# The last six units of a query projection in two load buffers, and expert rows 4 and 5 in the other two

## The reference

```python
def peer_ffn(h, w_q, keys_1, keys_2, u_table, v_table):
    q = jnp.dot(h, w_q).reshape(b, s, PEER_HEADS, 2, PEER_HALF)      # 2048 x 2048
    s1 = jnp.einsum('bshd,kd->bshk', q[:, :, :, 0], keys_1)          # 128 keys a side
    s2 = jnp.einsum('bshd,kd->bshk', q[:, :, :, 1], keys_2)
    v1, i1 = lax.top_k(s1, PEER_TOPK); v2, i2 = lax.top_k(s2, PEER_TOPK)
    ...                                                              # best 16 of the 256 pairs
    expert = jnp.take_along_axis(cand_index, top_pos, axis=-1)       # 8 heads x 16 a token
    gate = jax.nn.softmax(top_score.astype(jnp.float32), axis=-1)
    ...
        u = jnp.take(u_table, e_blk, axis=0)                         # a row of 2048 for each
        act = jax.nn.gelu(jnp.einsum('td,ted->te', h_blk, u), approximate=False)
        v = jnp.take(v_table, e_blk, axis=0)
        return jnp.einsum('te,ted->td', g_blk * act, v)
```

## Time and profile before

| | |
|---|---|
| median of 3 executions | 2711.09 us (2710.27 to 2713.92) |
| the profiled execution's own time | 2719.48 us |
| its span | 2717.0 us |
| TensorE busy | 2374.5 us (87%) |
| VectorE busy | 2061.6 us (76%) |
| ScalarE busy | 1009.8 us (37%) |
| mean DMA rate | 302 GB/s |
| chain that ended last, by engine | PE 61%, DVE 23%, DMA 7%, issue 5% |

### The profile page before, as it was taken

The page is one execution under the profiler, slowest core; times in us unless marked ns, Lnnn a source line. Parts: engine busy times, 40 slices in busy tenths (PEclk is TensorE's granted clock), DMA queues, the critical chain, the costliest instruction groups (busy, mean ns, idle before and its releaser), DMA issues.

```text
span 2717.0 us, 34317 instructions
## 1 busy us (share of the span) xinstructions
PE 2374.5 (87%) x12532; PEld 1891.1 (70%) x12532; DVE 2061.6 (76%) x2517; ACT 1009.8 (37%) x1428; POOL 869.9 (32%) x733
## 2 busy tenths in 40 slices
PE   4799999999999999999969867666666699999996
PEld 3688877888888887888859857656656664444442
DVE  7777779788888786554576999999999786665577
ACT  2254543344444444433343322227776750000000
POOL 0000011222222221000001566656666454444344
PEclk9799999999999999999989988887787799999998
DMA  9767669566666565555746899999999879999997
GB/s 385 292 215 243 226 228 358 208 213 215 217 217 215 207 215 193 207 189 186 258 178 230 353 419 419 419 419 388 404 407 388 344 256 414 413 413 414 414 413 277
DMA packets 144867, 819.86 MB, mean 302 GB/s; under 512 B 16680, under 2 KB 19360, under 8 KB 70480
## 3 DMA queue, kind: packets, MB, share of 16 engines
q0 software_dynamic: 93200, 477.21, 44.7%
q1 hardware_dynamic: 48480, 335.95, 33.3%
q10 hardware_dynamic: 3040, 4.68, 0.5%
HBM read 813.55 MB, written 4.23 MB: 301 GB/s over the span
## 4 chain that ended last, share of the span: by engine, by line
PE 61%; DVE 23%; DMA 7%; issue 5%; ACT 3%; POOL 1%; ACTq 0%; DVEq 0%; POOLq 0%
PE aux L1155 16%; DVE rrow L2151 9%; PE ps L706 8%; PE ps L707 8%; PE ps L712 7%; PE ps L731 4%; PE ps L732 4%; PE ps L737 4%; DMA rrow<-in_peer_u,acc 3%; DVE acc L1668 2%; DVE rrow_first L2151 1%; DVE wlo L1619 1%; PE aux L992 1%; DMA dskip<-in_D_skip 1%; DMA vden<-in_p_vd 1%
## 5 line engine op out<-in xcount | busy, mean ns | idle before, releaser
L1619 DVE TENSOR_TENSOR wlo<-raw,whi 128x2048 fp32r<-128x2048 f32 x216 | 499.6, 2314 | 292.4 <-ACT whi L1174 281.8
L1174 ACT ACTIVATE whi<-raw 128x2048 fp32r<-128x2048 f32 x216 | 412.1, 1910 | 664.1 <-PE ps L712 386.8
L2236 DVE SCALAR_TENSOR_TENSOR ps<-vrow,acc,ps 128x1024 f32<-128x1024 f32 x231 | 297.5, 1288 | 177.2 <-DMA vrow<-in_p_vg,acc 162.1
L2414 POOL DMA_INDIRECT rrow<-in_peer_u,acc x219 | 354.1, 1617 | 220.3 <-DVE dots L2151 115.2
L2151 DVE CUSTOM_DVE_ANT_0 rrow<-rrow,h 128x2048 f32<-128x2048 f32 x172 | 385.1, 2288 | 16.8 <-DMA rrow<-in_peer_u,acc 16.3
L2414 POOL DMA_INDIRECT vrow<-in_p_vg,acc x256 | 247.4, 966 | 265.3 <-DVE ps L2236 178.0
L2328 POOL DMA_DIRECT2D ada_in<-in_p_ada x128 | 69.3, 542 | 673.2 <-DVEq L1775 529.2
L1096 PE MATMUL aux<-hT,rT 128*128 128x128 f32 x1792 | 233.8, 294 | 37.1 <-ACT rT L1503 37.1
L731 PE MATMUL ps<-h_hi,whi 128*128 128x256 f32 x1040 | 264.6, 295 | 0.0
L1096 PEld LDWEIGHTS aux<-hT,rT 128*128 128x128 f32 x1792 | 226.7, 209 | 46.0 <-issue 31.7
L706 PE MATMUL ps<-whi,h_hi 128*128 128x512 f32 x576 | 235.1, 408 | 24.7 <-ACT whi L1174 24.1
(11 more groups left out here) (361 smaller groups left out, 4337.7 us busy)
## 6 DMA issues: line engine op xcount, KB each, us to landing
raw<-in_p_in SPq DMA_DIRECT2D x104, 1024.0 KB, 4.9
ada_in<-in_p_ada POOLq DMA_DIRECT2D x128, 512.0 KB, 4.8
vden<-in_p_vd SPq DMA_DIRECT2D x64, 1024.0 KB, 8.0
ada_in<-in_p_ada SPq DMA_DIRECT2D x32, 1024.0 KB, 10.1
raw<-in_p_so SPq DMA_DIRECT2D x32, 1024.0 KB, 4.7
raw<-in_p_mo SPq DMA_DIRECT2D x16, 1024.0 KB, 7.2
raw<-in_p_bc SPq DMA_DIRECT2D x16, 1024.0 KB, 6.4
raw<-in_p_mix SPq DMA_DIRECT2D x16, 1024.0 KB, 4.8
```

What stands on the lines that cost most here:

```text
L1174: F(whi[:, n % 2, :, 0:cols_], raw[:, n % 4, :, 0:cols_], ACT.Copy).then_inc(hi_ready, 1)
L1619: V.tensor_tensor(wlo[:, n % 2, :, 0:cols_], raw[:, n % 4, :, 0:cols_], whi[:, n % 2, :, 0:cols_].bitcast(F32), ALU.subtract).then_inc(lo_ ...
L2236: last = V.scalar_tensor_tensor(o, row, w, o, ALU.mult, ALU.add)
L2414: return G.indirect_dma_start(out=dst, out_offset=None, in_=table, in_offset=bass.IndirectOffsetOnAxis(ap=eid_all[:, r:r + 1], axis=0))
```

## The change

The last six units (`U_TWO` = 212) go round `raw` buffers 0 and 1 alone: 212, 214 and 216 in buffer 0, 213, 215 and 217 in buffer 1. So the loads of 214 to 217 wait for the remainder of two units before, and buffers 2 and 3 were last used by 210 and 211. The ring of eleven has its second and third place swapped: row 4 takes buffer 2 as before, row 5 takes buffer 3, and row 6 takes buffer 9. The gathers of rows 4 and 5 wait for the remainders of 210 and 211. SP's loop over the projection's loads is written out, 16 loads in a row, since the wait is no longer the same function of the loop's counter.

```diff
@@ -274,7 +274,7 @@
         SLOTS = (2, 3, 0, 1, 6, 4, 5, 7)
 
         WIDE = EARLY + 11 * (EARLY - 1 + ROWS)
-        wide = (2, ROWS + 1, 3, ROWS + 2, 0, 1, ROWS + 3, 6, 4, 5, 7)
+        wide = (2, 3, ROWS + 1, ROWS + 2, 0, 1, ROWS + 3, 6, 4, 5, 7)
 
         def row_slot(r):
 
@@ -562,9 +562,26 @@
                      "so": U_MIX, "mix": U_WQ, "h2": U_WQ, "wq": U_END, "all": U_END}[stop]
 
 
+        U_TWO = U_END - 6
+
+        def raw_slot(n):
+
+            return n % 4 if n < U_TWO else n % 2
+
+        def raw_before(n):
+
+            return n - 4 if n < U_TWO + 2 else n - 2
+
+        def last_unit_in(slot):
+
+            return max(n for n in range(U_END) if raw_slot(n) == slot)
+
         def full_count(base, j, i, per):
 
-            return 16 * ((base + j) // 4 + 1) + i * (16 * (per // 4))
+            n = base + j
+            if n >= U_TWO:
+                return 16 * sum(raw_slot(k) == raw_slot(n) for k in range(n + 1))
+            return 16 * (n // 4 + 1) + i * (16 * (per // 4))
 
         block = ctx.enter_context(nc.Block())
 
@@ -574,13 +591,13 @@
             def load(base, j, i, per, src):
 
                 n = base + j
-                sp_.wait_ge(lo_ready, i * per + (n + 1))
+                sp_.wait_ge(lo_ready, i * per + (raw_before(n) + 5))
                 sp_.sem_inc(held, 1)
                 kcs, width = src.shape[1:]
-                dst = raw[:, n % 4, :, 0:width] if kcs == 4 else \
-                    raw[:, n % 4].rearrange("p a b -> p (a b)")[:, 0:kcs * width].rearrange(
+                dst = raw[:, raw_slot(n), :, 0:width] if kcs == 4 else \
+                    raw[:, raw_slot(n)].rearrange("p a b -> p (a b)")[:, 0:kcs * width].rearrange(
                         "p (kc n) -> p kc n", kc=kcs)
-                sp_.dma_start(dst, src).then_inc(raw_full[n % 4], 16)
+                sp_.dma_start(dst, src).then_inc(raw_full[raw_slot(n)], 16)
 
             sp_.dma_start(con[:, :], a["consts"][:, 0:C_ALL]).then_inc(con_in, 16)
 
@@ -642,9 +659,8 @@
                     for u in range(8):
                         load(U_MIX, u, i, N_MIX, unit("p_mix", i * 8 + u))
             if on("wq"):
-                with sp_.Fori(0, 2) as i:
-                    for u in range(8):
-                        load(U_WQ, u, i, N_WQ, unit("p_pq", i * 8 + u))
+                for u in range(16):
+                    load(U_WQ, u, 0, 0, unit("p_pq", u))
             if not on("wq"):
                 for k in range(2):
                     load(last_unit, k, 0, 0, unit("p_in", k))
@@ -1168,10 +1184,10 @@
 
             def hi(base, j, i, per, cols_=W):
                 n = base + j
-                act.wait_ge(raw_full[n % 4], full_count(base, j, i, per))
+                act.wait_ge(raw_full[raw_slot(n)], full_count(base, j, i, per))
 
                 act.wait_ge(pe_used, i * per + (n + 1))
-                F(whi[:, n % 2, :, 0:cols_], raw[:, n % 4, :, 0:cols_], ACT.Copy).then_inc(hi_ready, 1)
+                F(whi[:, n % 2, :, 0:cols_], raw[:, raw_slot(n), :, 0:cols_], ACT.Copy).then_inc(hi_ready, 1)
 
             def hi_flat(base, j, i, per, count):
                 n = base + j
@@ -1616,7 +1632,7 @@
 
                 n = base + j
                 dve.wait_ge(hi_ready, i * per + (n + 1))
-                V.tensor_tensor(wlo[:, n % 2, :, 0:cols_], raw[:, n % 4, :, 0:cols_],
+                V.tensor_tensor(wlo[:, n % 2, :, 0:cols_], raw[:, raw_slot(n), :, 0:cols_],
                                 whi[:, n % 2, :, 0:cols_].bitcast(F32), ALU.subtract).then_inc(lo_ready, 1)
 
             def lo_flat(base, j, i, per, count):
@@ -2436,7 +2452,7 @@
                         pool.wait_ge(x1_ready, BLK)
                     elif slot < 4:
 
-                        pool.wait_ge(lo_ready, U_END + 1 + SLOTS.index(slot))
+                        pool.wait_ge(lo_ready, last_unit_in(slot) + 5)
                     else:
 
                         pool.wait_ge(pe_used, U_END + 1 + slot % 2)
```

## The result

The changed kernel takes 2720.24 us (median of 19 executions, 2714.52 to 2729.25), the kernel before, over as many executions, 2715.82 us (2710.27 to 2720.66). The medians are 4.4 us apart; the ratio, estimated from all executions, is 1.0020, 95% interval 1.0011 to 1.0028: slower by 3 to 7.6 us, where +0.7 had been forecast. The profiled execution of the changed kernel took 2729.25 us, 9.0 above the median; 3.2 us of its distance from the profile of before lie ahead of the projection already. So the two profiles are compared from one event to another, not by their spans.

What follows compares the result with a forecast made beforehand. The prediction saw a handover from TensorE's products through ScalarE's rounding to VectorE, then DMA and VectorE together in the row stage. Gathers nothing, loads +0.7 us, loop nothing: 2711.8 us on the 2711.09 median, range 2707 to 2717.

Steps and rivals of the forecast that it cites:

- +0.7: Projection's end: load 216 lands at 1500.9, making VectorE's remainder of 217 0.7 us late; near bounds 0 and +2.2.
- no gain from the early gathers: Row stage: gathers of rows 4 to 6 issued earlier bring nothing, since row 10 still waits for row 3's dot.
- Rival A: Row stage: three gathers of 2.5 us moved into idle DMA time save 7.5 us, giving 2703.6; 5 in 100.
- the time of load 214: Projection's loads: load 214, issued at 1478.39 among gathers, takes 9.0 us and lands at 1487.4, where 1487.12 was wanted.
- the written-out loop is free: SP's 16 loads in a row: constants replace register arithmetic on an engine that waits anyway; nothing.
- load 217 would find the engines nearly free: Projection's last load: issued from 1499.4, it runs nearly alone, takes 4.7 to 5.5 us and is in time.
- TensorE does not starve by this: TensorE in units 214 to 217: the late loads leave it no idle time; no cost.
- The prediction's own signs of being wrong: Changed profile: a load over 10 us or TensorE hole before unit 217; row 10 or first row wait clearly moved.
- rival B: Projection's loads: gathers crowd them out, a load takes 10.8 us, remainder of 217 5.8 us late; 2716.9; 10 in 100.
- the load of 215: Projection's loads: issued at 1485.93 with rows 4 and 5 beside it, takes 9.0 us, landing at 1494.9.
- One bound: Lower bound of the forecast loss: 0 if load 216 takes under 8.7 us.
- the rule that I weighed against the rows: DMA queues: by round-robin, two more gathers in their queue take nothing from a load; load 214 stays at 9.0 us.

Runs made afterwards that it cites:

- copies-first kernel: The changed kernel with both copies of slab 2's queries put ahead of unit 215 on ScalarE and VectorE; 1.0005 (0.9995 to 1.0015) of the kernel before.
- filled hole: The changed kernel with 24 unread products on TensorE ahead of its waits for slab 2's query copies; 1.0009 (0.9996 to 1.0021) of the kernel before.
- rotation only: The changed kernel's loads in two buffers, with the gathers waiting as in the kernel before; 0.9999 (0.9989 to 1.0009) of the kernel before.
- even only: Kernel before with only units 212, 214 and 216 sharing buffer 0 and row 4 gathered early; ratio 0.9996 (0.9985 to 1.0007).
- written out: Kernel before with only SP's loop over the projection's 16 loads written out; ratio 1.0004 (0.9993 to 1.0016).
- late copy: Kernel before with VectorE's copy of slab 2's queries put behind slab 1's score copy and row 2's dot; ratio 1.0020 (1.0009 to 1.0030).
- odd only: Kernel before with only units 213, 215 and 217 sharing buffer 1 and row 4 gathered early; ratio 1.0002 (0.9990 to 1.0014).
- before with copies first: Kernel before with both copies of slab 2's queries put ahead of unit 215; ratio 1.0008 (0.9996 to 1.0020).
- three kernels with the moved dot: Row 3's dot put behind the remainder of 216: in the kernel before 0.9984, with units 212, 214, 216 sharing a buffer 0.9991, with rows 9 and 10 swapped 0.9983.
- two changed kernels with copies first: The changed kernel with slab 2's query copies ahead of unit 215, alone 1.0005, and with row 3's dot behind the remainder of 216 1.0004 of the kernel before.

## Why the prediction was wrong

Right: no gain from the early gathers, and why. Row 10's wait of 4.00 us stayed, and VectorE's waits for rows did not shrink (17.2 us). Rival A at its full 7.5 us is refuted: the copies-first kernel has all three gathers early and is only 2.8 us longer in M, so by A it would be some 5 us below before, and its ratio is 1.0005 (0.9995 to 1.0015). A gain of 2 us or so from a single gather is not seen, but not excluded either. Right too: the time of load 214 (9.5 us for 9.0), that the written-out loop is free, and that load 217 would find the engines nearly free (4.8 us).

The forecast time was low for a second reason, which is no matter of the kernel: 2711.8 stood on a median of three executions, 2711.09, and over 19 the kernel before takes 2715.82. Of the 8.4 us between 2711.8 and 2720.24, 4.7 are this and 3.7 the loss that the prediction did not have.

**The step that failed** is "TensorE does not starve by this: ... the later units need only the rounding first". That held for the units. But TensorE's work between 214 and 215 is the scores of slab 2, and I followed from the late remainder to the next load and to the selection, not to the copy that stands behind it on VectorE. With my own times for the load (9.0 us, remainder done at 1499.2) the copies would have ended at 1499.9 where TensorE was ready at 1498.5: 1.4 us of idle time, twice the forecast. The rows that said so are the copy and the scores of the profile before, 0.8 us apart, which I did not read. What the runs showed in its place: TensorE idle for 2.89 us, and unit 217 late by 4.7 us. With the copies ahead of unit 215 the idle time is gone at an equally late load; with the copy late and no load late, it comes back (2.10 us). The prediction's own signs of being wrong, a load of over 10 us and a hole in TensorE's work before unit 217, both came; it had put them down to rival B alone.

**The size that failed** is the load of 215: 10.7 us, not 9.0. In flight beside it were four gathers, those of rows 2 to 5, and the end of load 214, which landed 2.0 us after 215's issue. Without the two early gathers it took 8.7 us, without load 214 beside it and with one early gather 7.1. How it went is seen in the queues, first from 1490.5 to 1492.0, then from 1492.5 to 1496.5:

```profile
q0 software_dynamic: 94, 0.65, 102.6%
...
q1 hardware_dynamic: 110, 0.90, 54.0%
q0 software_dynamic: 110, 0.77, 46.4%
```

The load moved nothing until over 3 us after its issue, while the gathers had all engines, and then had half of them. The load of 214 did the same: nothing for over 3 us, and 51.4% from 1485.0 to 1488.5. So far 9.0 was a fair size for both. What 215 took on top lies at its end: nearly all its bytes had passed by 1497.4, and it landed at 1499.63. What held the rest stays open.

Rival B had 10.8 us for a load, close to the 10.7 measured, but from a share of 29.1% in which, as the prediction itself said, the time before the first packet is counted. Its total (+5.8) is near the measured one, but by another path: it made load 217 and the remainder of 217 late, and load 217 was in time. The right total from the wrong place is luck. The forecast's own +0.7 was worked out on VectorE's path by the load of 216; that load took 7.5 us, and that path had 2.94 us to spare. One bound was also slipped: the load of 216 alone would have had to take under 8.3 us, not 8.7, for a loss of 0.

**What I had no term for** is the clock: of the 1.3 us on the scores the filled hole shows 1.05 to be the clock's, and the 0.5 on the products behind them.

As to the rule that I weighed against the rows (the Trainium skill, "DMA: Bandwidth & Descriptors", "Queues, rings and completion order": the engines go round-robin between queues that have work): load 214, with the gathers' queue beside it, took 9.5 us with the two early gathers behind in that queue and 9.5 without them (rotation only), which agrees; so do the near halves above. What the rule means for load 215 I had not worked out: of the two gathers added, the load paid as long as they kept the other queue busy. In rotation only that queue was all but empty 2.5 us after 215's issue, and the load had the engines to itself.

## What to carry to other kernels

When a buffer's slack is cut, follow the late instruction on *every* engine that waits for it, and then each instruction queued behind it there, up to the other engines that wait for those: the loss was in a 0.7 us copy that needed nothing from the late load. Look for copies and small steps that stand behind a wait they do not need; moving them ahead of it cost nothing that these runs can tell (1.0008, 0.9996 to 1.0020, in the kernel before) and keeps a margin. And moving a transfer into idle DMA time gained nothing that could be seen here, where the gathers behind it wait for something else; ask first what the first wait of the full stretch is released by.

## What the runs showed of the hardware

- TensorE's granted clock held (scores 2.02 us) after 0.91 us of idle time in this stage, and was 0.68 and 0.62 of full over the 3.4 and 3.5 us behind 2.10 and 2.89 us of idle time, between its two levels (1.2 and 2.4 GHz). Filling the time with unread products kept it.
- A 1 MB load of SP took 4.7 to 4.8 us with no gather in flight. Issued with three or four gathers in flight (changed kernel, 214 and 215) it moved nothing for over 3 us and then had about half of the engines (51.4% and 54.0%), and took 9.5 and 10.7 us.
- At the last scores of the projection TensorE is idle for 3.28 us in most kernels here, and the scores behind took 2.02 us in some (before, even only, written out, filled hole) and 2.7 to 3.4 in others (changed, late copy, rotation only, odd only, before with copies first) with the same 3.3 us ahead. With 1.6 us ahead (the three kernels with the moved dot and no late load of 215) they took 2.02 each time; with 4.83 and 4.12 us ahead (the two changed kernels with copies first) 3.75 and 2.86. The two granted clocks, of before and of before with the copies first:

```profile
1519.86:1524.36 4.50, 2.06 (x17) 1.93 (x18) 4.50 (x8) 1.35 (x2) 3.89 (x3) 1.00 0.94 370
```

```profile
1513.57:1518.07 4.50, 3.40 (x16) 3.24 (x16) 3.79 (x7) 0.05 (x1) 3.89 (x3) 0.62 0.95 380
```

What decides between them stays open; at the same idle time it is worth up to 0.9 us of M, and it comes in kernels without a late load too (before with copies first), so it is not counted as the change's.
